# One hybrid attention and expert step on one core: VectorE's first quad ahead of a late head, and expert choices made later

## The reference, cut to what matters

```
xn = rms_norm(x) * g_mix;  z = xn @ w_in            # q, k, v of A and B, two gates
merged = sigmoid(ga) * (A @ w_a) + sigmoid(gb) * (B @ w_b)   # A dilated windows, B local, 8 heads each
h = x + merged @ w_o
hn = rms_norm(h) * g_ffn
# PEER, 8 retrieval heads:
q = hn @ w_pq;  s = q . sub_keys                    # 2 x 128 scores per head and row
top 16 of each half -> sums of pairs -> top 16 -> 16 expert numbers e, gates = softmax
act = gelu(hn . u[e]);  y = h + sum_e (gate * act) * v[e]    # u, v: 16384 rows of 1024
out = rms_norm(y) * g_final
```

## Time and profile before

| | us |
|---|---|
| median of 3 runs | 1932.74 (1930.5 to 1933.16) |
| the profiled execution | 1932.0 |
| its span | 1930.2 |
| TensorE busy | 1405.9 |
| VectorE busy | 1216.0 |
| GpSimd busy | 1067.7 |
| ScalarE busy | 369.8 |

### The profile page before, as it was taken

How to read it: one execution, slowest core, us unless ns; L and a number is a source line. 1 busy time by engine, 2 the same in 40 slices (tenths; PEclk the granted TensorE clock), 3 DMA queues, 4 the chain that set the end, 5 groups by cost and what they waited for, 6 DMA issues and landing times.

```text
span 1930.2 us, 18803 instructions
## 1 busy us (share of the span) xinstructions
PE 1405.9 (73%) x5438; PEld 643.6 (33%) x5438; DVE 1216.0 (63%) x3335; ACT 369.8 (19%) x906; POOL 1067.7 (55%) x1082
## 2 busy tenths in 40 slices
PE   8999988885894779664998666666656576654657
PEld 5443433453442344221334233223323233321111
DVE  1015343268766768666766788787877878978541
ACT  2112433222222222111111111211111221111000
POOL 3010000036566677675656777767777777766763
PEclk9999988987797899777999688978778888877668
DMA  9989996879899899999999999999999999999995
GB/s 324 369 306 351 366 308 227 268 244 326 332 399 398 335 350 406 359 401 399 368 397 361 403 409 409 409 409 410 409 409 409 409 409 406 401 386 409 410 409 217
DMA packets 227304, 710.66 MB, mean 368 GB/s; under 512 B 21289, under 2 KB 46793, under 8 KB 227177
## 3 DMA queue, kind: packets, MB, share of 16 engines
q0 software_dynamic: 166912, 612.40, 82.2%
q1 hardware_dynamic: 60288, 97.05, 14.4%
HBM read 704.84 MB, written 72.65 MB: 403 GB/s over the span
## 4 chain that ended last, share of the span: by engine, by line
DMA 36%; PE 27%; issue 14%; POOL 11%; DVE 9%; ACT 1%; SPq 0%; DVEq 0%; POOLq 0%; ACTq 0%
DMA XS<-in_peer_u_dram,e_all 14%; DMA arena<-in_peer_u_dram,e_all 11%; DMA GT<-in_peer_u_dram,e_all 5%; POOL WR L650 5%; PE bank L927 5%; PE bank L1038 5%; DMA WR<-in_peer_v_dram,arena 4%; PE bank L1055 4%; POOL XS L650 3%; PE bank L1154 3%; PE bank L1133 3%; DVE XS L1436 2%; POOL arena L650 2%; PE bank L1175 1%; DMA WR<-out_dram 1%
## 5 line engine op out<-in xcount | busy, mean ns | idle before, releaser
L1038 PE MATMUL bank<-WR,arena 128*64 128x512 f32 x1720 | 513.9, 739 | 294.7 <-DMA WR<-in_peer_v_dram,arena 271.6
L650 POOL DMA_INDIRECT WR<-in_peer_v_dram,arena x430 | 420.5, 978 | 196.7 <-issue 128.8
L650 POOL DMA_INDIRECT XS<-in_peer_u_dram,e_all x258 | 274.0, 1062 | 230.7 <-issue 85.2
L1038 PEld LDWEIGHTS bank<-WR,arena 128*64 128x64 f32 x1720 | 148.3, 167 | 607.4 <-issue 550.7
L1436 DVE SCALAR_TENSOR_TENSOR XS<-XS,bank 128x1024 f32<-128x1024 f32 x144 | 174.9, 1221 | 94.4 <-DMA XS<-in_peer_u_dram,e_all 90.6
L1436 DVE SCALAR_TENSOR_TENSOR GT<-GT,bank 128x1024 f32<-128x1024 f32 x126 | 152.5, 1220 | 81.3 <-DMA GT<-in_peer_u_dram,e_all 78.5
L1436 DVE SCALAR_TENSOR_TENSOR XS<-XS,GT 128x1024 f32<-128x1024 f32 x114 | 138.3, 1225 | 88.3 <-DMA XS<-in_peer_u_dram,e_all 87.4
L650 POOL DMA_INDIRECT GT<-in_peer_u_dram,e_all x126 | 122.8, 975 | 50.5 <-issue 34.2
L650 POOL DMA_INDIRECT arena<-in_peer_u_dram,e_all x128 | 126.7, 990 | 40.8 <-issue 38.7
L1055 PE MATMUL bank<-WR,XS 128*128 128x512 f32 x256 | 120.7, 626 | 14.5 <-ACT GT L793 14.2
L1436 DVE SCALAR_TENSOR_TENSOR arena<-arena,bank 128x1024 f32<-128x1024 f32 x90 | 109.9, 1221 | 10.7 <-DMA arena<-in_peer_u_dram,e_all 7.4
(11 more groups left out here) (228 smaller groups left out, 2055.5 us busy)
## 6 DMA issues: line engine op xcount, KB each, us to landing
out_dram<-in_cache_a_k_dram POOLq DMA_DIRECT2D x8, 4064.0 KB, 54.6
out_dram<-in_cache_a_v_dram POOLq DMA_DIRECT2D x8, 4064.0 KB, 55.1
WR<-in_w_in_dram SPq DMA_DIRECT2D x8, 2048.0 KB, 25.2
GT<-in_w_peer_q_dram SPq DMA_DIRECT2D x14, 1024.0 KB, 16.4
WR<-in_w_out_dram SPq DMA_DIRECT2D x6, 2048.0 KB, 18.1
WR<-in_peer_v_dram,arena POOLq DMA_INDIRECT x430, 14.6
WR<-in_w_branch_a_dram SPq DMA_DIRECT2D x6, 1024.0 KB, 9.1
WR<-in_w_branch_b_dram SPq DMA_DIRECT2D x6, 1024.0 KB, 13.0
```

The source lines that it names most:

```text
L650: nc.gpsimd.indirect_dma_start(dst, None, table, bass.IndirectOffsetOnAxis(ap=idx, axis=0))\
L1038: last = nc.tensor.matmul(b[c][R * j:R * j + R, :], diag[v % 4][:, s % 4, :], V[V_AT[s]][:, c * CHUNK:(c + 1) * CHUNK], start=False, stop= ...
```

## The change

Tile 0's heads after the first stand four positions apart instead of three: at 24, 27, 31, 35 and so on to 51, where they stood at 24, 27, 30 to 45. Tiles 1, 2 and 3 begin six positions later, the sample five. On SyncE the load of `kept_weights(0)` and the wait ahead of it stand behind the answer of tile 0 and the reload of the sample's x, since `query(1,4)` is now in position 71 instead of 65. On VectorE the first quad's four products stand ahead of the last attention piece of position 28, `("att", 1, 7)`, whose VectorE part is the masked reduction of head 9 of tile 1 (`scored(1, 9)`, line 1250), instead of at the head of position 29. GpSimd's order and TensorE's quads are as before.

```diff
 def head_at(t, h):
     if t == 0:
-        return 24 + 3 * h
-    return SLOT0 + {1: 20, 2: 51, 3: 75, SAMPLE: 99}[t] + {1: 4, SAMPLE: 2}.get(t, 3) * h
+        return 24 if h == 0 else 27 + 4 * (h - 1)
+    return SLOT0 + {1: 26, 2: 57, 3: 81, SAMPLE: 104}[t] + {1: 4, SAMPLE: 2}.get(t, 3) * h
...
             query_weights(PH + 4)
             sp.wait_ge(S["onorm"], 2 * TILES - 1)
             kept_weights(5)
-            filled(sp, "query", 1, 4, 0)
-            kept_weights(0)
             sp.wait_ge(S["onorm"], 2 * TILES)
             kept_weights(6)
...
             answer(0)
             x_again(SAMPLE)
+            filled(sp, "query", 1, 4, 0)
+            kept_weights(0)
             out_weights(2, 0)
...
+            late_head = [piece for piece in PLAN[SLOT0 - 1] if piece[0] == "att"][-1]
             for pieces in PLAN:
                 for stage, *at in pieces:
+                    if (stage, *at) == late_head:
+                        quad(0)
                     if stage == "quad":
-                        quad(at[0])
+                        if at[0]:
+                            quad(at[0])
```

## The result

The changed kernel takes 1975.33 us in the median of 4 runs (1971.87 to 1979.33), the kernel before 1932.82 in runs beside it: ratio 1.0233, 95% interval 1.0211 to 1.0255. It is slower by 42.5 us; I had said slower by 24, with 1971 as the upper end. The profiled execution took 1971.87 us (span 1970.1), 39.9 more than that of before.

The account below looks back on a forecast made before the run. From the first gather on the kernel was taken as a DMA stream with holes. Tile 1's 24.8 us plus 0 for the rest gave 25 us on 1932.0, so 1957; range 1948 to 1964, with rivals on its side 1937 to 1971.

Parts of the forecast that it names:

- the sum over tile 1's heads: Tile 1's picks directly before their gathers: eight heads, 4.1 us each at an ordinary boundary, corrected by place, 24.8 us together.
- Head 4: Tile 1, at 1002 us: TensorE fully busy, so much of the delay is absorbed; 2 us, between 0 and 4.1.
- Head 3: Tile 1, gap 6.7 us: 2.1 us of tile 3's branch work stands before the pick; 4.7 us.
- Head 2: Tile 1: an ordinary boundary like head 1, with 4.5 us from gather issue to landing; 4.1 us.
- Head 5: Tile 1, gap already 7.6 us because weight loads fill the queue; 1.7 us.
- SyncE's order: kept_weights(0) moved later on SyncE, needed only from position 86; 0 us, bound +5.
- Tile 0 and the early quads: Tile 0's choices four positions apart: same work, spread; -2 to 0 us, taken as 0, bounds -10 and +5.
- the early term: Early part of the kernel: DMA holes of 390 to 660 us add up to 31 us, the most it can give.
- The first quad: Products ahead of head 9's reduction in tile 1 cover a VectorE wait; gain 1.1 us, bounds 0 and 2.
- Tiles 2, 3 and the sample: Their later picks still stand far enough ahead of their gathers; 0 us, bounds +4 for tile 2, +3 for the sample.
- Full delay and lost queue depth: Rival: tile 1's heads pay in full, landings take 5.7 us, the queue stays shallow; 35 us, 1967 us, chance 0.25.
- The other tests: Signs in the trace: DMA stream full after tile 1; wrong if gathers wait for products or v buffers, not the cast.

Follow-up runs that it names:

- e5: The changed kernel with each pick sorted right behind the quad, ahead of branches and output pieces on VectorE; ratio 1.0237 to the kernel before.
- e9: The changed kernel once more, on a slower chip in one series with the kernel before; ratio 1.0232.
- e11: The kernel before with SyncE's edit alone, kept_weights(0) and its wait moved later, run a second time; ratio 0.9996.
- e14: The changed kernel with tile 1's heads three positions apart and tiles 2, 3 and the sample back in their old places; ratio 1.0112.
- e10: The kernel before, unchanged, traced on a slower chip; a single execution of 2055.6 us.
- e1: The kernel before with only VectorE's first quad moved ahead of the late head; ratio 1.0005.
- e15: The kernel before, unchanged, compared against itself; ratio 1.0006.
- e17: e14 with the kept_weights(0) load and its wait issued ahead of tile 0's answer; ratio 1.0049.
- e18: e17 with tile 0's choices three positions apart again, as in the kernel before; ratio 1.0084.

## Why the prediction was wrong in size

**The step that failed is the sum over tile 1's heads.** It took one local delay, the pick's, times the heads, and corrected it by what filled each place in the kernel *before*. By how much the time from the first product of the quad before to the first product of the head's quad grew, predicted and measured from the two timelines:

| head | 0 | 1 | 2 | 3 | 4 | 5 | 6 | 7 | sum |
|---|---|---|---|---|---|---|---|---|---|
| predicted | 0 | 4.1 | 4.1 | 4.7 | 2 | 1.7 | 4.1 | 4.1 | 24.8 |
| measured | -1.0 | 3.7 | 8.1 | 6.6 | 10.9 | 3.2 | 4.3 | 4.0 | 39.7 |

Heads 0, 1, 6 and 7 are right within 1.1 us. Head 4 alone is 8.9 us off. I priced it at 2 because TensorE was busy 20.00 of 20.00 us there and "so much is absorbed". Nothing was. A pick queued on VectorE behind an addition that waits for TensorE does not hide in the wait, it inherits it (7.76 us), and passes it to GpSimd. That wait could not be read off the kernel before, where it was 1.69 us; the plan after shows it, with tile 1's own query product moved in front. Head 3, 1.9 off, has the same cause with 3.2 us of waiting. I had counted the branch pieces' work there and not their wait. That the waits ahead of the pick are the mis-sized step at these two heads is shown by e5, which sorts the pick in front of them and shortens these two gaps, by 4.3 and 6.1 us against e9, and no other by more than 0.3. That the moved query products make TensorE late is read from the traces and not tested by a run.

Head 2 is 4.0 off: its gather was issued into queues with SyncE's loads in them, with 7.2 us to landing instead of 4.5. Head 5 is 1.5 off. The other quads of 32 to 64 gave 6 us back, so the stretch lost 33.7 us from quad 31.

**SyncE's order, taken as 0 (bound +5).** I weighed the load by its own deadline, position 86, "far off", and looked at what it passes. What stands right *behind* its new place is 2 x 2 MB of output weights needed at once. Alone it costs nothing (e11); with later queries it is part of the rest that e14 showed. How much of the changed kernel's 39.7 us it makes, beside the pick waits in the same quads, was not run by itself. Its trace shows little of it. TensorE's first output matmuls of tile 2 wait for VectorE there, and only the second ones wait for weights, about as long as in e10 (3.32 us), where the load has not moved:

```profile
982.69 7.10 PE L1154 MATMUL bank<-WR,arena 128*128 128x512 f32 x16 [2.33 <-DVE GT L1522]
...
996.68 10.12 PE L1154 MATMUL bank<-WR,arena 128*128 128x512 f32 x16 [3.31 <-DMA WR<-in_w_out_dram]
```

**Tile 0 and the early quads, taken as 0 (-10 to +5).** Measured +6.0 us at quad 31, just over the upper bound; how much of it is tile 0's spacing is open. The lead of 16.7 us at quad 18 had turned into that by quad 31. The share of 390 to 660 us did not move from 0.91. The text said "if the first 660 us are more than 8 us shorter at the same quad, the early term was undervalued"; that test was badly put, since bytes can be postponed across its end.

**The first quad.** Taken as 1.1 us; e1's ratio of 1.0005 shows none, within an interval of 0.3%. VectorE of the changed kernel, the reduction ahead of the products and the first of them:

```profile
401.67 0.48 DVE L1250 CUSTOM_DVE_ANT_0 PP<-bank,GF,nsink 128x256 f32<-128x256 f32 x1 [0.95 <-PE bank L957]
...
402.08 1.22 DVE L1436 SCALAR_TENSOR_TENSOR XS<-XS,GT 128x1024 f32<-128x1024 f32 x1
```

In the earlier trace rows it was 1.07 us before the last reduction; that one is covered now, the 0.95 us before the reduction ahead of it is not.

**Tiles 2, 3 and the sample**, taken as 0: 0.9996, right.

**The rivals.** "Full delay and lost queue depth" (1967) came nearest, mostly for another reason. It rightly left head 4 unhidden, but at 4.1 us. Its longer landings were seen at head 2 alone, and after tile 1 nothing runs dry, as the flat 39.7 us shows.

**The tests.** The gathers waited for the cast by name and the share fell to 0.95. The gaps after quads 35, 55 and 59 are 8.9, 9.5 and 9.0 us, near the 9 to 10 foretold; the one after quad 39 is 12.0, which was a sign of the wrong size. The first product stands at 402.1 us and not 405; the attention before it ran ahead in that execution, as the late head's reductions show (401.67 us against 404.43). The other tests spoke of the mechanism, not of its size.

**A reading.** In the earlier trace rows slices 15 and 17 stand at nine tenths; the smaller sags are at 3, 11 and 14. No term of the sum hangs on it.

## What to carry to other kernels

A stage moved to the last position before its consumer costs each delay that stands ahead of it *in that position*. So price each occurrence by the queue in its new place, not by how much the old place was covered, and write out the other engines' order in the new plan too, since the move can bring them work just ahead. When a load moves, look at what is issued right behind it: here the output weights came up to 9.4 us later. An early lead at one mark is worth nothing until the bytes moved by then are compared.

## What was unexpected in the hardware

The same program took 1929 to 1933 us in two series and 2028 to 2038 us in the other four, each of these on a chip of its own. Of the 127 us between the spans of e15 and e10, 78 lie after quad 64, where the DMA engines carry little but gathers. One stretch, e15, then e10 (the same kernel on a slower chip), and what GpSimd waited for in e10's:

```profile
1300.00:1600.00 300.00, 195.40 (x863) 90.32 (x862) 240.91 (x694) 50.54 (x139) 225.96 (x234) 0.85 1.03 409
```
```profile
1300.00:1600.00 300.00, 178.05 (x722) 81.51 (x721) 202.64 (x613) 45.19 (x120) 193.73 (x201) 0.76 0.92 348
```
```profile
POOL WR L650 <- remote: 27.7, 9, 4.7
```

The DMA share falls from 1.03 to 0.92 and the rate from 409 to 348 GB/s, and GpSimd waits nine times for something that the profile calls remote; in e15 it has no such wait in this stretch. The cause was not found. On these chips one kernel's runs lie 1 to 2% apart, and differences of less than half a per cent, as between e17 and e18, are not to be had.

The other number is the share of a direct load beside gathers: 2 MB of weights took 20.4 us, 103 GB/s, while the DMA engines moved some 400 GB/s in all.
